# Output projection of a two-block transformer kernel: the order of VectorE's level steps, modulation products and of three TensorE pieces among the weight chunks

## The reference

```python
mod = silu(c) @ w_ada + b_ada                     # six vectors: shift1, scale1, gate1, shift2, scale2, gate2
h = rms_norm(x) * (1 + scale1) + shift1
proj = h @ w_in                                   # attention q, k, v and HGRN2 q, f, i, g
attn = rms_norm(dilated_attention(...))           # 8 heads
hg = rms_norm(hgrn2(...)) * silu(g)               # 8 heads, a gated linear recurrence
mix = concat([attn, hg]) @ w_out                  # the output projection, 2048 x 2048
x = x + gate1 * mix
h2 = rms_norm(x) * (1 + scale2) + shift2          # then the feed-forward layer, and the second block
```

## Time and profile before

| | us |
|---|---|
| median of 3 runs | 2456.74 |
| lowest and highest run | 2454.43, 2457.46 |
| span of the profiled execution | 2453.7 |
| TensorE busy | 2362.5 (96%) |
| VectorE busy | 1593.8 (65%) |
| ScalarE busy | 1036.6 (42%) |
| GpSimd busy | 47.8 (2%) |

### The profile page before, as it was taken

The page is one execution under the profiler, slowest core; times in us unless marked ns, Lnnn a source line. Parts: engine busy times, 40 slices in busy tenths (PEclk is TensorE's granted clock), DMA queues, the critical chain, the costliest instruction groups (busy, mean ns, idle before and its releaser), DMA issues.

```text
span 2453.7 us, 27892 instructions
## 1 busy us (share of the span) xinstructions
PE 2362.5 (96%) x10954; PEld 1969.7 (80%) x10954; DVE 1593.8 (65%) x1282; ACT 1036.6 (42%) x874; POOL 47.8 (2%) x55
## 2 busy tenths in 40 slices
PE   4899999988999999999999999999999999999999
PEld 3777888777888888888887888878888888888887
DVE  7878989966566666656568556556555555555554
ACT  2255553434333333343344556664443333333432
POOL 1011000000000000000000000000000000000000
PEclk9999999999999999999999999999999999999999
DMA  9988997653677667655554645435555555555553
GB/s 352 371 295 319 354 318 273 224 175 117 224 242 243 234 229 238 225 193 176 188 189 142 219 155 161 164 124 168 184 188 187 191 193 185 191 188 188 188 188 103
DMA packets 235129, 520.30 MB, mean 212 GB/s; under 512 B 9705, under 2 KB 10162, under 8 KB 232370
## 3 DMA queue, kind: packets, MB, share of 16 engines
q1 hardware_dynamic: 234352, 519.15, 62.7%
q10 hardware_dynamic: 706, 0.17, 0.0%
HBM read 517.19 MB, written 2.10 MB: 212 GB/s over the span
## 4 chain that ended last, share of the span: by engine, by line
PE 88%; DVE 5%; DMA 2%; ACT 2%; issue 1%; DVEq 1%; POOL 1%; ACTq 0%; SPq 0%
PE PS L256 27%; PE PS L258 27%; PE PS L257 27%; DMA ada_raw<-in_w_ada_dram 2%; PE PS L1599 2%; PE PS L1638 1%; DVE w_lo L246 1%; DVE ada_acc L1096 1%; PE PS L1573 1%; PE PS L303 1%; ACT w_hi L242 1%; POOL rstd L570 1%; PE PS L1583 1%; ACT A_hi L339 0%; DVE MS L1041 0%
## 5 line engine op out<-in xcount | busy, mean ns | idle before, releaser
L246 DVE TENSOR_TENSOR w_lo<-raw,w_hi 128x2048 fp32r<-128x2048 f32 x392 | 897.8, 2291 | 698.2 <-ACT w_hi L242 692.7
L242 ACT ACTIVATE w_hi<-raw 128x2048 fp32r<-128x2048 f32 x392 | 751.6, 1918 | 1170.7 <-PE PS L258 1158.8
L256 PE MATMUL PS<-w_hi,A_hi 128*128 128x512 f32 x2112 | 838.7, 397 | 9.9 <-DVE A_lo L358 5.4
L258 PE MATMUL PS<-w_hi,A_lo 128*128 128x512 f32 x2112 | 827.6, 392 | 0.0
L257 PE MATMUL PS<-w_lo,A_hi 128*128 128x512 f32 x2112 | 827.5, 392 | 0.0
L256 PEld LDWEIGHTS PS<-w_hi,A_hi 128*128 128x128 f32 x2112 | 400.2, 190 | 92.6 <-DVE A_lo L358 5.0
L258 PEld LDWEIGHTS PS<-w_hi,A_lo 128*128 128x128 f32 x2112 | 399.7, 189 | 84.4
L257 PEld LDWEIGHTS PS<-w_lo,A_hi 128*128 128x128 f32 x2112 | 400.2, 190 | 81.5 <-issue 1.0
L256 PE MATMUL PS<-w_hi,H_hi 128*128 128x512 f32 x1024 | 401.6, 392 | 1.6 <-issue 1.3
L258 PE MATMUL PS<-w_hi,H_lo 128*128 128x512 f32 x1024 | 398.9, 390 | 0.0
L257 PE MATMUL PS<-w_lo,H_hi 128*128 128x512 f32 x1024 | 398.4, 389 | 0.0
(11 more groups left out here) (265 smaller groups left out, 1111.7 us busy)
## 6 DMA issues: line engine op xcount, KB each, us to landing
raw<-in_w_ff_dram SPq DMA_DIRECT2D x128, 1024.0 KB, 5.3
raw<-in_mlp_w_in_dram SPq DMA_DIRECT2D x64, 1024.0 KB, 5.5
raw<-in_mlp_w_out_dram SPq DMA_DIRECT2D x64, 1024.0 KB, 5.0
raw<-in_w_in_dram SPq DMA_DIRECT2D x56, 1024.0 KB, 8.2
X<-in_w_ada_dram SPq DMA_DIRECT2D x96, 512.0 KB, 5.7
raw<-in_sb_w_qkv_dram SPq DMA_DIRECT2D x48, 1024.0 KB, 5.1
ada_raw<-in_w_ada_dram SPq DMA_DIRECT2D x32, 1024.0 KB, 9.8
raw<-in_w_out_dram SPq DMA_DIRECT2D x16, 1024.0 KB, 7.4
```

What stands on the lines that cost most here:

```text
L242: act.activation(w_hi[:, j, :, :], raw[:, j, :, :], ACT.Copy).then_inc(hi_rdy, 1)
L246: dve.tensor_tensor(w_lo[:, j, :, :], raw[:, j, :, :], w_hi[:, j, :, :].bitcast(F32), ALU.subtract).then_inc(lo_rdy, 1)
L256: pe.matmul(bank(pair + t), h, w_hi[:, j, k, :], start=first, stop=False)
L258: mm = pe.matmul(bank(pair + t), l, w_hi[:, j, k, :], start=False, stop=last)
```

## The change

It moves work and adds none but a few drains of VectorE.

- VectorE copies level 0 before the `split_lo` of slot 15 of the last projection group, that is ahead of the last two chunks' low parts and of the gate multiplication.
- `LEVEL_SLOTS` takes all pieces out of slots 55 to 57 and one out of slot 59. The products that stood in slots 55 to 58 now stand in 58 to 61, which are behind the level steps of positions 2 to 5.
- VectorE's order for positions 0 to 8 is written out by hand. The growing step to level 6 is followed by the copy of level 5, the steps to levels 7 and 8 come each as soon as the level before is there, with modulation products and a `split_lo` between them. Two more calls of `split_lo` move behind the last steps.
- `chunk` gets a hook `between`, called after the first half of the tokens. TensorE's level 6 stands inside chunk 5, level 8 inside chunk 6, and the last turn inside chunk 8. Level 7 follows chunk 5, and the product with the values follows chunk 6.
- ScalarE's order follows: level 6 before the `split_hi` at position 5, levels 7 and 8 before that at position 6, the square and the last turn's copies one position earlier.
- SyncE loads the pieces of a slot behind its chunk for positions 0 to 9, and the wait for the whole ring with the load of x moves from position 7 to position 12.
- The split of `hg_stage` into `level_grow` and `level_copy` adds a drain to each of their calls, in the first group of heads too.

```diff
 OUT_EARLY, WO_EARLY = 9, 9
+OUT_WIDE = {5: (6,), 6: (7, 8)}
 ADA_EARLY = ADA_BLOCKS - D // NC_
...
 HG1_SLOT = CH * (OUT0 - 4)
-LEVEL_SLOTS = (range(HG1_SLOT, HG1_SLOT + 7),)
+LEVEL_SLOTS = (range(HG1_SLOT, HG1_SLOT + 7),) + 2 * (range(CH * OUT0 - 1, CH * OUT0 + 2),) + (range(CH * OUT0 + 3, CH * OUT0 + 4),)
...
-        def chunk(pe, B, j, pair, hi, lo, start, stop, half=None):
+        def chunk(pe, B, j, pair, hi, lo, start, stop, half=None, between=None):
...
                     mm.then_inc(half, 1)
+                if between is not None and t == 0:
+                    between()
             mm.then_inc(chunk_done, 1)
-        def square_chunk(pe, B0, order, pos, take, half=None):
+        def square_chunk(pe, B0, order, pos, take, half=None, between=None):
...
             chunk(pe, B0 + pos // CH, pos % CH, pairs[b % 3], lambda i, t: A_hi[:, CH * k + i, P * t:P * t + P],
-                  lambda i, t: A_lo[:, CH * k + i, P * t:P * t + P], pos == mine[0], pos == mine[-1], half)
+                  lambda i, t: A_lo[:, CH * k + i, P * t:P * t + P], pos == mine[0], pos == mine[-1], half, between)
...
                     load(B, j, v[:, k, :, b, :])
-                    if ada and B <= OUT0 + 1:
+                    if ada and pos < 2 * CH + 2:
                         for q in ada_pieces(CH * (B - 1) + j):
                             ada_load(q)
-                    if ada and pos == 2 * CH - 1:
-                        for slot in range(CH * (OUT0 + 1), CH * (OUT0 + 2) + 2):
-                            for q in ada_pieces(slot):
-                                ada_load(q)
+                    if ada and pos == CH * 3:
                         sp.wait_ge(ring_used, 8 * ADA_EARLY)
...
             hg_stage(1, OUT0 - 4, 0)
-            for pos in range(OUT_EARLY):
-                hg_stage(1, OUT0 - 4, pos + 1)
-                if pos == OUT_EARLY - 1:
+            for pos in range(OUT_EARLY - 1):
+                for l in OUT_WIDE.get(pos, ()):
+                    wide_copy(1, l)
+                if pos == OUT_EARLY - 2:
                     hg_stage(1, OUT0 - 4, 11)
...
             turn_act(act, 1, gmix, **mix_part(3))
-            for pos in range(OUT_EARLY, CH * 4):
+            for pos in range(OUT_EARLY - 1, CH * 4):
                 split_hi(act, OUT0 + 1 + pos // CH, pos % CH)
...
+            def gate_mul(g):
+                dve.wait_ge(g_sig, g + 1)
+                dve.tensor_tensor(GN[:, :, :], PS[:, 2:4, :], GN[:, :, :], ALU.mult).then_inc(pair_read[1], 1)
+            def level_grow(g, s):
+                d()
+                dve.wait_ge(lv_mm, NLV * g + s)
+                grow(WIDTHS[s], g, lv_rdy)
+            def level_copy(g, l):
+                w = WIDTHS[l]
+                d()
+                dve.wait_ge(lv_mm, NLV * g + l + 1)
+                b = level_bank(l, g)
+                both = AM[:, 0:2, :, :].rearrange("p r h s -> p (r h) s")
+                src = PS[:, b:b + 2, :].rearrange("p b (h s) -> p (b h) s", s=P)
+                if l == 0:
+                    dve.tensor_tensor(both, src, ident[:, :].unsqueeze(1).to_broadcast([P, 2 * GH, P]),
+                                      ALU.mult).then_inc(lv_cp, 1)
+                else:
+                    m = lv_mask[:, LEVELS.index(w), :].unsqueeze(1).to_broadcast([P, 2 * GH, P])
+                    dve.copy_predicated(both, m, src).then_inc(lv_cp, 1)
+                d()
...
                 if s == 1:
-                    dve.wait_ge(g_sig, g + 1)
-                    dve.tensor_tensor(GN[:, :, :], PS[:, 2:4, :], GN[:, :, :], ALU.mult).then_inc(pair_read[1], 1)
+                    gate_mul(g)
                 d()
                 if 2 <= s < NLV:
-                    dve.wait_ge(lv_mm, NLV * g + s)
-                    grow(WIDTHS[s], g, lv_rdy)
+                    level_grow(g, s)
                 if 0 <= s - 1 < NFINE:
-                    l = s - 1
-                    w = WIDTHS[l]
-                    dve.wait_ge(lv_mm, NLV * g + l + 1)
-                    b = level_bank(l, g)
-                    both = AM[:, 0:2, :, :].rearrange("p r h s -> p (r h) s")
-                    src = PS[:, b:b + 2, :].rearrange("p b (h s) -> p (b h) s", s=P)
-                    if l == 0:
-                        dve.tensor_tensor(both, src, ident[:, :].unsqueeze(1).to_broadcast([P, 2 * GH, P]),
-                                          ALU.mult).then_inc(lv_cp, 1)
-                    else:
-                        m = lv_mask[:, LEVELS.index(w), :].unsqueeze(1).to_broadcast([P, 2 * GH, P])
-                        dve.copy_predicated(both, m, src).then_inc(lv_cp, 1)
-                    d()
+                    level_copy(g, s - 1)
                 if s == 11:
...
                         turn_dve(dve, 1, gmix, **mix_part(s - 13))
+                    if kind == "hg" and idx == 1 and s == 15:
+                        level_copy(1, 0)
                     split_lo(dve, B0 + (s - 1) // CH + 1, (s - 1) % CH)
...
-            for pos in range(OUT_EARLY):
-                hg_stage(1, OUT0 - 4, pos + 1)
-                if pos:
-                    split_lo(dve, OUT0 + 1 + (pos - 1) // CH, (pos - 1) % CH)
+            def out_lo(x):
+                split_lo(dve, OUT0 + x // CH, x % CH)
+            gate_mul(1)
+            for pos in range(1, 5):
+                level_grow(1, pos + 1)
+                level_copy(1, pos)
+                out_lo(pos + 3)
                 if pos in (1, 3):
...
                 ada_slot(CH * OUT0 + pos)
+            level_grow(1, 6)
+            level_copy(1, 5)
+            out_lo(8)
+            level_grow(1, 7)
+            ada_adds(CH * OUT0 + 5)
+            level_grow(1, 8)
+            out_lo(9)
+            ada_collects(CH * OUT0 + 5)
+            out_lo(10)
             hg_stage(1, OUT0 - 4, 11)
             turn_dve(dve, 1, gmix, **mix_part(3))
+            out_lo(11)
             for b in range(3):
...
+            def last_mix():
+                pe.wait_ge(o_out, 2)
+                turn(1, MIX, **mix_part(3))
+            inside = {5: lambda: hg_stage(1, 6), 6: lambda: hg_stage(1, 8), 8: last_mix}
+            after = {0: 1, 1: 2, 2: 3, 3: 4, 4: 5, 5: 7, 6: 10}
             for pos in range(CH * 4):
...
                 if pos == OUT_EARLY:
-                    pe.wait_ge(o_out, 2)
-                    turn(1, MIX, **mix_part(3))
                     pe.wait_ge(a_lo, 2 * KT // 2)
...
                     mod_columns(D // NC_, ADA_EARLY, SEL[:, :])
-                square_chunk(pe, OUT0, OUT_ORDER, pos, take, out_half if pos == CH * 4 - 1 else None)
-                if pos < OUT_EARLY:
-                    hg_stage(1, pos + 1 if pos < OUT_EARLY - 1 else 10)
+                square_chunk(pe, OUT0, OUT_ORDER, pos, take, out_half if pos == CH * 4 - 1 else None, inside.get(pos))
+                if pos in after:
+                    hg_stage(1, after[pos])
                 if pos in (2, 4):
...
                         gate_spread(b, b, E0f[:, NC_ * (b % 2):NC_ * (b % 2 + 1)])
```

## The result

| | before, us | after, us |
|---|---|---|
| median (4 runs each) | 2456.38 | 2440.39 |
| lowest and highest run | 2454.43, 2457.46 | 2437.41, 2441.08 |
| span of the profiled execution | 2453.7 | 2435.4 |
| time of the profiled execution | not in the records | 2437.41 |

The ratio is 0.9931, with a 95% interval of 0.9918 to 0.9944: about 16 us faster by the medians, 14 to 20 us by the interval, and so beyond the 4.9 us that a measurement of this kernel can't tell from no change. The forecast was 2438.6 for the median and 2435.6 for the span. The time of each run lies 2.0 us above its own span (2437.41 and 2435.4).

The account below looks back on a forecast made before the run. TensorE was taken as the bound, with 88% of the chain that ended last. Gains 7.07 + 11.22 - 0.1 = 18.2, less 0.1 for drains, gave 18.1 us: 2456.74 to 2438.6 us, range 2434.5 to 2445 (8 in 10).

Parts of the forecast that it names:

- The two stalls: TensorE idle in the output projection: 4.41 us ahead of level 1, 5.66 us at the last turn, each with slow clock.
- the second term: From the product with the values to chunk 10: moving TensorE's pieces inside chunks gains 11.22 us, less what stays uncovered.
- the first term: From the end of chunk 0 to level 2's start: 14.31 us holding 7.24 of work, gain 7.07 us.
- level 0 first: VectorE copies level 0 ahead of low parts and gate multiplication, so level 1 needn't wait; gain 7.07 us.
- modulation products later: Seven products leave slots 55 to 57 and 59 for 58 to 61, where VectorE has free time; cost 0.
- ahead of level 1 stand no other new waits: Check on the early level 0 copy: done near 463.5 us, 4.2 us before level 1 asks for it.
- The covers: TensorE work over other engines' chains: level 6 keeps 0 to 0.8 us, last turn 2.1; `A_lo` waits 0.1.
- The turn inside the chunk: Last turn's eight transposes inside chunk 8 take 0.79 us; by the skill's clock rule about 1.6, gain 0.8 less.
- SyncE: Loads of chunks 8, 9, 10 at about 475, 483, 492 us, x about 510; cost 0, cover over 10 us.
- rival D: Slower than before: SyncE's waits in the ring delay a weight load until TensorE stops, 2464 us; chance 0.04.
- Rival A: A stall stays or returns, likeliest at the last turn: 3 us wait plus slow clock, 6.2 in all, 2444.8 us; chance 0.08.
- Rivals B and C: B: only the first stall goes, 2449.7 us, 0.04; C: projection ends earlier but what follows doesn't, 2456 us, 0.04.

## Why the prediction was right, and which step of it was wrong

**The two stalls and their sizes: right.** The first was priced at 7.07 and is worth 7.27 (135.16 - 127.89), of which 7.11 lie ahead of the last turn; the second was priced at 11.22 and is worth 10.92 (127.89 - 116.97). Behind the same second stall the slow part differed by 1.16 us between kernels (50.95 to 52.11), so the second term is not known more closely than that, and a sum that comes within 0.1 us of the measured stretch is partly luck. Reading each stall as "start to start, less the work at full clock" took in the slow clock behind it without a rule for it. It costs a shown wait fully, too: in these runs a wait of 1.82 us in brackets made the stretch 2.08 longer, and one of 1.66 made it 1.90 longer, since the last matmul's record (0.39 us long, where the next one starts after 0.23) covers the first 0.16 of each wait, and the level with the chunk behind the wait took about 0.1 longer than elsewhere.

**Which edit carries the first term: wrong.** The prediction gave 7.07 to the part "level 0 first" and wrote "cost 0" under "modulation products later", with VectorE's free time in the stretch as the reason. Free time in a window of 56 us says nothing of the queue in the first ten. In fact the late products are worth 5.43 us alone and 6.17 in the changed kernel, the early copy 1.37 alone and 2.08 in the changed kernel. The sum came out since both edits were made. With the copy alone the same working would have forecast a gain of 7.07, and the kernel is not faster (1.0002). The step that fails is the check that I made for level 1 only, "ahead of level 1 stand no other new waits": with the products in their old slots VectorE is late at the next three levels. For the early copy it is the price of what comes behind it in the queue that was left out.

**The covers: right in sign, and near in size.** Level 6 was given 0 to 0.8 and had about 0.8; a step with a copy took 2.88 (500.43 to 503.31) against the 2.72 of the earlier trace rows, so the two added drains cost 0.16 a step together, under the 0.1 to 0.2 each that I took as the upper side. The last turn was given 2.1 and had 1.74: from the product's start to the norm's first step passed 4.58 us (516.75 to 521.33) in place of the 4.1 forecast. `A_lo` ended at 530.78 (529.12 and 1.66) and chunk 9 started at 531.22, so 0.1 for it was 0.1 too much.

**The turn inside the chunk.** The turn took 0.79 (527.61 to 528.40) at a granted clock of 1.00. By "TensorE: Matmul & The Clock Gate", Part 4, of the Trainium skill, it would have been 1.6, an estimate of 0.8 us more; the trace after doesn't agree with that, as the earlier trace rows didn't.

**SyncE: right to the microsecond.** Its queue after:

```profile
474.78 0.38 SPq L409 DMA_DIRECT2D raw<-in_w_out_dram  x1
...
483.34 1.42 SPq L409 DMA_DIRECT2D raw<-in_w_out_dram  x1
...
492.48 13.52 SPq L409 DMA_DIRECT2D raw<-in_w_out_dram  x3
510.06 0.37 SPq L465 DMA_DIRECT2D X<-in_x_dram  x1
```

The load of chunk 8 was forecast for 475 (474.78), chunk 9's for 483 (483.34), chunk 10's for 492 (492.48) and x for 510 (510.06). No load is among the releasers of TensorE or ScalarE in the stretch, so rival D had nothing to stand on.

**Rival A, a stall that stays.** It didn't occur. Its price was tested: a wait of 3.23 us costs 5.07, where the prediction had 6.2 for 3. Rivals B and C fall with the windows of the changed kernel: from chunk 10 on the chunks moved forward as a whole (40.18 us from its start to the transposes before, 40.17 after), and the idle time ahead of the feed-forward layer is 6.45 against 6.46 us. The first group's drains cost nothing: TensorE shows no wait there after either.

**Where the median lies.** 2440.39 is 1.8 above the forecast, while the span hit it within 0.2. That hit is partly luck: the profiled run was the fastest of the four (2437.41), and the spans of the other three are 2438.3 to 2439.1. Of the 3.04 us that I added to the span, 2.0 lie around the span in every run, and the other 1.0 only says which execution was profiled. The runs of either kernel spread by 3 to 4 us. The change in the median (16.0 us) is smaller than that in the stretch (18.19) by an amount that the runs' spread covers; for these two traces nothing behind the stretch accounts for more than 0.5 us (1858.08 before, 1858.57 after, from the first transposes to the end).

## What to carry to other kernels

Price a stall from start to start and subtract the work at full clock; then ask of every edit by itself what stands in the releasing engine's queue, up to the third or fourth step behind the one that you free. A piece that starts a chain through other engines goes as early as its inputs allow, and the piece that ends the chain goes inside a chunk, so that half a chunk lies over what follows it. A wait that is only shifted along a queue shows up again at the next step of the chain: look there before taking it as gained.

## What the runs showed of the hardware that I had not expected

**The length of a wait doesn't decide alone whether the clock falls.** It stayed at 1.00 through a wait of 3.14 us ahead of a level (two runs of the kernel with early products), and fell about 0.6 us behind a wait of 2.19 us that stood right behind the last turn (two runs). With a wait of 3.23 us ahead of the last turn it fell about 0.4 us behind the wait in one run and 0.2 us before its end in the other. It fell during waits of 4.41, 5.66 and 6.75 us. Each pair of runs agrees on whether the clock falls; two runs of a kernel don't exclude chance.

**The work around the wait doesn't decide alone either.** In four kernels TensorE waits the same 5.66 us between the product with the values and the last turn. Counted from the end of the product's last record, the clock fell 2.3 us into that wait with the late products alone, 3.7 with TensorE's pieces between the chunks as before, 4.0 before, and 4.7 with the early copy alone. What else takes part was not taken apart and stays open.

**The fall can come after the wait.** With the turn between the chunks, TensorE ran at 1.00 through the wait and for about 0.6 us of chunk 9 before its matmuls went from 0.23 to 0.43 us from start to start. The slow part's length varied too. From the last turn's start to the clock's return it was 8.6 us before and 6.9 to 9.3 in the other kernels with the second stall, 3.8 and 3.2 in the two runs with ten extra instructions and about 3 in that with 17.

**The start of the stretch moves by kernel.** Level 0 started between 459.49 and 463.39 us in the traces, although the engines' work ahead of it differs by no more than a few drains. Two runs of one kernel lay 0.02 to 0.62 us apart. The granted clock from 60 to 110 us differed (0.97 before, 0.76 after, 0.73 with early products), but it does not set the start: the kernel after, at 0.76, started 0.6 us earlier than the kernel before at 0.97, and the two runs with ten extra instructions, at 0.93 and 0.76, started within 0.14 us of each other. The cause stays open.
